# Rotary rotation of query and key tiles in halves of 512 tokens, with three half-size partner buffers

## What is computed

```python
def _layer(x, cond, pl, lambda_init, rope=None, ctx_kv=None):
    ada = (jax.nn.silu(cond) @ pl['w_ada'] + pl['b_ada']).astype(x.dtype)
    sh1, sc1, g1, sh2, sc2, g2 = jnp.split(ada[:, None, :], 6, axis=-1)
    h = x * (1 + sc1) + sh1
    y, k, v = _token_mixers(h, pl, lambda_init, rope, ctx_kv)
...
    z = h @ pl['w_in']
...
def _rot_half(x, cos, sin):
    x1, x2 = jnp.split(x, 2, axis=-1)
    return jnp.concatenate([x1 * cos - x2 * sin, x2 * cos + x1 * sin], -1)
...
        q = _apply_axial_rope(q, rope)
        k = _apply_axial_rope(k, rope)
```

## Time and profile before

| what | value |
|---|---|
| median of 3 runs | 4157.65 us (4147.48 to 4159.18) |
| the profiled execution | 4153.43 us, span 4151.6 us |
| TensorE matmul busy | 3590.7 us (86% of the span) |
| TensorE weight load busy | 2981.8 us (72%) |
| VectorE busy | 2400.7 us (58%) |
| ScalarE busy | 1084.8 us (26%) |
| GpSimd busy | 1542.0 us (37%) |
| mean granted TensorE clock | 0.930 |

### The profile page before, as it was taken

How to read it: one execution, slowest core, us unless ns; L and a number is a source line. 1 busy time by engine, 2 the same in 40 slices (tenths; PEclk the granted TensorE clock), 3 DMA queues, 4 the chain that set the end, 5 groups by cost and what they waited for, 6 DMA issues and landing times. The chain is left out here.

```text
span 4151.6 us, 49240 instructions
## 1 busy us (share of the span) xinstructions
PE 3590.7 (86%) x18590; PEld 2981.8 (72%) x18590; DVE 2400.7 (58%) x2950; ACT 1084.8 (26%) x2000; POOL 1542.0 (37%) x759
## 2 busy tenths in 40 slices
PE   6899897887679999999849997788686999999992
PEld 3577675776568888888737776677565888888882
DVE  3245546775755555555653654677566555555557
ACT  2212112673241111111241111267414111111115
POOL 1526566202423233323344656720133333233234
PEclk7799998998889999999969998999897999999996
DMA  5677544433011111111037654453300111111101
GB/s 201 213 248 214 178 115 158 101 100 107 21 31 36 36 41 41 36 36 41 7 108 229 196 168 138 147 140 99 101 26 21 41 37 35 41 41 32 40 11 51
DMA packets 286902, 380.69 MB, mean 92 GB/s; under 512 B 17743, under 2 KB 203069, under 8 KB 285406
## 3 DMA queue, kind: packets, MB, share of 16 engines
q1 hardware_dynamic: 212370, 219.71, 18.4%
q10 hardware_dynamic: 74316, 157.86, 11.2%
HBM read 286.28 MB, written 82.84 MB: 89 GB/s over the span
## 5 line engine op out<-in xcount | busy, mean ns | idle before, releaser
L665 POOL TENSOR_TENSOR RH<-RAW,ONE 128x1024 fp32r<-128x1024 f32 x256 | 502.2, 1962 | 1805.7 <-PE PS L774 830.2
L774 PE MATMUL PS<-HH,RH 128*128 128x512 f32 (+1 forms) x2784 | 626.1, 369 | 200.6 <-DVE HL L1805 73.7
L774 PEld LDWEIGHTS PS<-HH,RH 128*128 128x128 f32 x2784 | 479.5, 195 | 320.3 <-issue 110.7
L667 POOL TENSOR_TENSOR RL<-RAW,RH 128x1024 fp32r<-128x1024 f32 x256 | 641.2, 2505 | 20.0
L774 PE MATMUL PS<-HL,RH 128*128 128x512 f32 (+1 forms) x2784 | 596.6, 357 | 0.0
L774 PE MATMUL PS<-HH,RL 128*128 128x512 f32 (+1 forms) x2784 | 590.2, 354 | 0.0
L2045 DVE TENSOR_TENSOR SB<-RB 128x512 f32<-128x512 f32 (+1 forms) x192 | 204.2, 1064 | 639.9 <-ACT RB L1688 639.9
L2061 DVE SCALAR_TENSOR_TENSOR XT<-PS,ADA,XT 128x512 f32<-128x512 f32 (+1 forms) x768 | 474.5, 655 | 140.1 <-PE PS L1183 134.7
L774 PEld LDWEIGHTS PS<-HL,RH 128*128 128x128 f32 x2784 | 475.7, 192 | 76.4
L774 PEld LDWEIGHTS PS<-HH,RL 128*128 128x128 f32 x2784 | 469.6, 190 | 72.6
L1688 ACT ACTIVATE RB<-PS 128x512 f32<-128x512 f32 (+1 forms) x192 | 101.2, 527 | 1480.9 <-PE PS L774 1479.7
(11 more groups left out here) (234 smaller groups left out, 5011.1 us busy)
## 6 DMA issues: line engine op xcount, KB each, us to landing
RAW<-in_w_mlp_dram SPq DMA_DIRECT2D x128, 512.0 KB, 3.9
ADW<-in_w_ada_dram ACTq DMA_DIRECT2D x80, 512.0 KB, 5.5
RAW<-const_dram SPq DMA_DIRECT2D x68, 512.0 KB, 3.9
RAW<-in_w_in_dram SPq DMA_DIRECT2D x44, 512.0 KB, 5.1
x_scratch<-XT SPq DMA_DIRECT2D x4, 2560.0 KB, 12.3
z_scratch<-ZST ACTq DMA_DIRECT2D x40, 256.0 KB, 3.2
QH<-q_hi SPq DMA_DIRECT2D x32, 320.0 KB, 9.4
QL<-q_lo SPq DMA_DIRECT2D x32, 320.0 KB, 10.5
```

The lines of the kernel that those rows point to most:

```text
L665: nc.gpsimd.tensor_tensor(RH[:, s, :], RAW[:, p, :], ONE[:].broadcast_to([128, 1024]), ALU.mult).then_inc(hi_split.sem, 1)
L667: nc.gpsimd.tensor_tensor(RL[:, s, :], RAW[:, p, :], RH[:, s, :].bitcast(F32), ALU.subtract)\
L774: mm = pe.matmul(out, w[:, s, k * 128:(k + 1) * 128], m(k), start=(n == 0 and k == 0), stop=(n == 2 and k == KT - 1))
```

## The change

ZSW was one buffer of 1024 tokens; it becomes three of 512. Of every query or key tile the partner features are now moved in two halves, each by eight DMAs of 16 partitions by 512 tokens: the first half after the evacuation of strip q = 0 or 1, in the second strip (that is, right after the second evacuation), the second half after the third strip's. Each group of eight stands ahead of modulation in its strip. GpSimd rotates each half by three operations over 512 tokens. The waits for rotations count halves. Two semaphores are saved elsewhere: the two new_v_stored become one, and a wait on lam_known becomes a link of a chain.

```diff
--- before.py
+++ after.py
@@ -272,7 +272,7 @@
 
     st = Stack(XT_O, WS)
     ZRAW = st.take("ZRAW", [128, 3, T])
-    ZSW = st.take("ZSW", [128, LS])
+    ZSW = st.take("ZSW", [128, 3, 512])
     ZHI = st.take("ZHI", [128, 2, T], F32R)
     ROPE = st.take("ROPE", [128, 2, LS])
     st = Stack(XT_O, WS)
@@ -380,10 +380,9 @@
         c_hi = signal("c_hi", 1)
         c_lo = signal("c_lo", 1)
         c_stored = signal("c_stored", 2 * 16)
-        qk_partner = signal("qk_partner", 8 * 8 * 16)
-        rope_sin = signal("rope_sin", 8)
-        rope_cos = signal("rope_cos", 8)
-        rope_done = signal("rope_done", 8)
+        qk_partner = [signal(f"qk_partner{p}", len(range(p, 16, 3)) * 8 * 16) for p in range(3)]
+        rope_parts = signal("rope_parts", 2 * 16)
+        rope_done = signal("rope_done", 16)
         qk_hi = signal("qk_hi", 8)
         qk_lo = signal("qk_lo", 8)
         zhi_stored = [signal(f"zhi_stored{p}", 4 * 16) for p in range(2)]
@@ -392,7 +391,7 @@
         k_copied = signal("k_copied", 4)
         new_k_stored = [signal(f"new_k_stored{p}", 2 * 16) for p in range(2)]
         v_stored = [signal(f"v_stored{p}", len(range(p, TT, 4)) * 16) for p in range(4)]
-        new_v_stored = [signal(f"new_v_stored{p}", 16) for p in range(2)]
+        new_v_stored = signal("new_v_stored", 2 * 16)
         conv_in = signal("conv_in", 6 * 48 + 2 * 64)
         conv_done = signal("conv_done", 8, 1)
         conv_stored = signal("conv_stored", 8 * 32, 16)
@@ -424,7 +423,6 @@
         hy_stored = signal("hy_stored", 4 * 16, 16)
 
         lam_ready = signal("lam_ready", 1)
-        lam_known = signal("lam_known", 1)
         qk_in = [signal(f"qk_in{s}", 2 * 12 * 16) for s in range(2)]
         v_in = [signal(f"v_in{s}", 2 * 2 * 16) for s in range(2)]
         s_psum = signal("s_psum", 2 * G)
@@ -681,13 +679,16 @@
                 x, z = n % 3, n + 1
                 if n == 0:
                     pool.wait_ge(rope_in.sem, rope_in.at(l, 16))
-                pool.wait_ge(qk_partner.sem, qk_partner.at(l, z * 8 * 16))
-                nc.gpsimd.tensor_tensor(ZSW[:], ZSW[:], ROPE[:, 1, :], ALU.mult).then_inc(rope_sin.sem, 1)
-                nc.gpsimd.tensor_tensor(ZRAW[:, x, 0:LS], ZRAW[:, x, 0:LS], ROPE[:, 0, :], ALU.mult)\
-                  .then_inc(rope_cos.sem, 1)
-                pool.wait_ge(rope_sin.sem, rope_sin.at(l, z))
-                pool.wait_ge(rope_cos.sem, rope_cos.at(l, z))
-                nc.gpsimd.tensor_tensor(ZRAW[:, x, 0:LS], ZRAW[:, x, 0:LS], ZSW[:], ALU.add).then_inc(rope_done.sem, 1)
+                for half in range(2):
+                    u, cols = 2 * n + half, slice(512 * half, 512 * half + 512)
+                    pool.wait_ge(qk_partner[u % 3].sem, qk_partner[u % 3].at(l, (u // 3 + 1) * 8 * 16))
+                    nc.gpsimd.tensor_tensor(ZSW[:, u % 3, :], ZSW[:, u % 3, :], ROPE[:, 1, cols], ALU.mult)\
+                      .then_inc(rope_parts.sem, 1)
+                    nc.gpsimd.tensor_tensor(ZRAW[:, x, cols], ZRAW[:, x, cols], ROPE[:, 0, cols], ALU.mult)\
+                      .then_inc(rope_parts.sem, 1)
+                    pool.wait_ge(rope_parts.sem, rope_parts.at(l, 2 * u + 2))
+                    nc.gpsimd.tensor_tensor(ZRAW[:, x, cols], ZRAW[:, x, cols], ZSW[:, u % 3, :], ALU.add)\
+                      .then_inc(rope_done.sem, 1)
 
             def split_rotated(l, n):
                 x, z = n % 3, n + 1
@@ -1395,17 +1396,19 @@
                             S.activation(to.rearrange("p t v -> p (t v)"), PS[:, 7, 0:8], ACT.Copy)\
                              .then_inc(ada_placed.sem, 1)
 
-                def partners(i):
-
-                    act.wait_ge(z_evac.sem, z_evac.at(l, 3 * (Z_Q + i) + 3))
-                    act.wait_ge(rope_done.sem, rope_done.at(l, i))
+                def partners(i, half):
+
+                    u, cols = 2 * i + half, slice(512 * half, 512 * half + 512)
+                    act.wait_ge(z_evac.sem, z_evac.at(l, 3 * (Z_Q + i) + half + 1))
+                    act.wait_ge(rope_done.sem, rope_done.at(l, max(u - 2, 0)))
                     for p in range(0, 128, 16):
                         o = p + 16 if p % 32 == 0 else p - 16
-                        act.dma_start(ZSW[p:p + 16, :], ZRAW[o:o + 16, i % 3, 0:LS]).then_inc(qk_partner.sem, 16)
+                        act.dma_start(ZSW[p:p + 16, u % 3, :], ZRAW[o:o + 16, i % 3, cols])\
+                           .then_inc(qk_partner[u % 3].sem, 16)
 
                 def high_parts(i):
 
-                    act.wait_ge(rope_done.sem, rope_done.at(l, i + 1))
+                    act.wait_ge(rope_done.sem, rope_done.at(l, 2 * i + 2))
                     act.wait_ge(zhi_stored[i % 2].sem, zhi_stored[i % 2].at(l, 16 * (i // 2)))
                     S.activation(ZHI[:, i % 2, :], ZRAW[:, i % 3, :], ACT.Copy).then_inc(qk_hi.sem, 1)
 
@@ -1467,6 +1470,8 @@
                                 act.wait_ge(zlo_stored[i % 3].sem, zlo_stored[i % 3].at(l, 16 * (i // 3)))
                             S.activation(ZRAW[:, i % 3, t0:t0 + tn], z, ACT.Copy, scale=SCALE if i < HEADS else 1.0)\
                              .then_inc(z_evac.sem, 1)
+                        if i >= 0 and q:
+                            partners(i, q - 1)
                         modulation(u)
                         if q == 0 and i > 1:
                             store_low(i - 2)
@@ -1484,8 +1489,6 @@
                                 prompt_keys(i - HEADS - 1)
                             if i > 0:
                                 high_parts(i - 1)
-                    if i >= 0:
-                        partners(i)
                     if i > 0:
                         store_high(i - 1)
                     if n in UNIT_AT:
@@ -1506,7 +1509,7 @@
                     act.dma_start(v_d[t], VRAW[:, t % 4, :]).then_inc(v_stored[t % 4].sem, 16)
                     if t >= ST:
                         act.dma_start(new_v[0, l, (t - ST) * 128:(t - ST + 1) * 128].rearrange("p m d -> p (m d)"),
-                                      VRAW[:, t % 4, :]).then_inc(new_v_stored[t % 2].sem, 16)
+                                      VRAW[:, t % 4, :]).then_inc(new_v_stored.sem, 16)
 
                 for t in range(TT):
                     keep_value(t)
@@ -1536,7 +1539,7 @@
                     act.wait_ge(u_psum.sem, u_psum.at(l, t + 1))
                     S.activation(MH[:, t, 256:512], PS[:, 4 + t % 2, 0:256], ACT.Copy).then_inc(u_hi.sem, 1)
 
-                for stored in (*v_stored, *new_v_stored):
+                for stored in (*v_stored, new_v_stored):
                     act.wait_ge(stored.sem, stored.at(l, stored.per_layer))
                 for j in range(TT):
                     b0 = 2 * (j % 2)
@@ -1721,7 +1724,7 @@
                 act.wait_ge(y_stored[p].sem, 16 * TT // 2)
             for p in range(2):
                 act.wait_ge(new_k_stored[p].sem, new_k_stored[p].at(DEPTH - 1, 2 * 16))
-                act.wait_ge(new_v_stored[p].sem, new_v_stored[p].at(DEPTH - 1, 16))
+            act.wait_ge(new_v_stored.sem, new_v_stored.at(DEPTH - 1, 2 * 16))
 
 
         @block.vector
@@ -1943,8 +1946,7 @@
 
                 dve.wait_ge(lam_exp.sem, lam_exp.at(l, 1))
                 C.link(V.tensor_tensor(LAMS[:, 0:1], LAMS[:, 3:4], LAMS[:, 2:3], ALU.subtract))
-                V.tensor_tensor(LAMC[:, 2:3], LAMS[:, 0:1], LAMC[:, 0:1], ALU.subtract).then_inc(lam_known.sem, 1)
-                dve.wait_ge(lam_known.sem, lam_known.at(l, 1))
+                C.link(V.tensor_tensor(LAMC[:, 2:3], LAMS[:, 0:1], LAMC[:, 0:1], ALU.subtract))
 
                 def maxima(g, m):
                     h, t, k0, kn = item(g)
```

## The result

| | before | after the change |
|---|---|---|
| median of 9 runs each | 4156.82 us (4147.48 to 4159.37) | 4164.44 us (4159.38 to 4170.47) |
| the profiled execution | 4153.43 us, span 4151.6 | 4159.38 us, span 4157.6 |
| mean granted TensorE clock | 0.930 | 0.930 |
| query and key tiles, layer 0 | 143.0 us | 160.6 us |
| query and key tiles, layer 1 | 135.6 us | 131.9 us |

The ratio to the kernel before is 1.0024, with a 95% interval of 1.0013 to 1.0034: slower by 7.6 us between the medians, a third of the 23 us that were forecast, and inside the 0.3% that I had called no change. Small as it is, the interval leaves out 1, so the loss is real. The last two rows are the stage of the change, from the first matmul of tile 10 to the first of the values (before: 303.6 to 446.6 us and 2302.0 to 2437.6 us). It lost 17.6 us in layer 0 and gained 3.7 us in layer 1.

The account below looks back on a forecast made before the run. TensorE was taken to bound the kernel, its waits coming from ScalarE. Layer 0 +25 us (+19.8 idle, +5 clock) and layer 1 -1 gave +24: 4177 from the profiled execution, 4181.7 from the median, so 4180, range 4150 to 4204.

Parts of the forecast that it names:

- The loop and its end: Query/key tiles: rotation, ZHI, evacuation, issue and landing loop in 16.9 us a tile; the change ends ZHI's 4.5 us wait.
- The issue at 5.0 us a group: ScalarE's issue of eight half-length partner DMAs costs 5.0 us, as at double length, with bounds of 2.8 and 6.3 us.
- Both rivals with a cheaper issue: ScalarE's partner issue: near 0.45 us each, 4158 us, chance 0.2; or 0.35 us each, 4146 us, chance 0.12.
- the estimate of 0.43 us: ScalarE's DMA issue by the skill's 512 cycles at 1.2 GHz: 3.4 us a group, sum near 0.
- The queue did not fill up: Rival on ScalarE's partner groups: 6.3 us each, about +36 us in layer 0, +12 in layer 1, 4204; chance 0.13.
- The places in layer 0: TensorE's idle places at strips 33 to 50: sum 27.0 us plus 2.4 of hand-over, against 9.6 before, +19.8.
- the two of 0.7 us: Layer 0, weights for strip 37 and again after the turn at 46: TensorE waits another 0.7 us each.
- Hand-overs of 2.4 us: Layer 0: about 0.3 us of hand-over added at each of eight places where TensorE waits.
- 0.6 + 5.0: ScalarE in layer 0: an evacuation of 0.6 us, then a group's issue of 5.0, before its other duties.
- 0.6 + 5.0 + 1.2 + 0.4 + 5.0: ScalarE's longer sums: evacuation 0.6, group 5.0, ZHI 1.2, evacuation 0.4, second group 5.0 us, before what TensorE awaits.
- The clock: TensorE in layer 0: 2.5 us lost per idle time of 2.9 us or more, four against two, +5 us.
- within 0.3%: Whole kernel: a difference under 12.5 us can't be told from none; chance 0.20.

Follow-up runs that it names:

- modulation first: The changed kernel with modulation(u) ahead of the group of eight partner DMAs in each strip: 4142.97 us, 0.9967 of the kernel before.
- the same halves without ScalarE's burden: The changed kernel with both partner groups of a tile issued by SyncE, high_parts waiting for the third evacuation: 4128.26 us, 0.9938 of the kernel before.
- groups wait for their own strip: The changed kernel with each group waiting for the evacuation of the strip it stands behind (half + 2 for half + 1): 4184.23 us, 1.0068 of the kernel before.
- the kernel with 16 DMAs a tile: The kernel before with each partner DMA cut in two over its tokens, all sixteen after the third strip: 4203.83 us, 1.0113 of the kernel before.

## Why the prediction was wrong

Wrong in size, right in sign and in cause: the groups' place ahead of the adaLN copies costs time in layer 0, as the run with modulation first shows. Point by point:

- **The loop and its end**: right. ZHI's waits for GpSimd fell from 77.8 to 6.5 us, and the same halves without ScalarE's burden are 28.4 us faster than before.
- **The issue at 5.0 us a group**: right, 611 ns each. Both rivals with a cheaper issue are out, and with them the estimate of 0.43 us from the Trainium skill's "DMA: Bandwidth & Descriptors" and "Advanced Engine Details and Errata": the runs give 611 ns on ScalarE for 16 partitions at 2 KB and at 4 KB a row, and 612 ns for 32 at 2 KB. The queue did not fill up either: the groups of layer 0 took 5.0 to 5.8 us.
- **The places in layer 0**: the eight waits stand where they were forecast; of the ten places priced, the two of 0.7 us had none, six were too large and two too small. Hand-overs of 2.4 us in all had been added.

| place | forecast | the change | groups wait for their own strip |
|---|---|---|---|
| weights, strip 33 | 5.0 | 2.7 | 6.3 |
| placing, strip 35 | 2.0 | 1.6 | 2.2 |
| weights, strip 37 | 0.7 | none | 1.5 |
| turn, strip 38 | 3.1 | 2.9 | 1.9 |
| turn, strip 42 | 4.3 | 3.4 | 5.2 |
| weights, strip 45 | 2.2 | 1.5 | 2.9 |
| turn, strip 46 | 4.7 | 2.8 | 1.8 |
| placing, strip 47 | 2.0 | 2.3 | 5.0 |
| weights, strip 49 | 0.7 | none | none |
| turn, strip 50 | 2.3 | 2.5 | 2.9 |
| hand-overs, transposes | 2.4 | | 0.6 |
| sum | 29.4 | 19.7 | 30.3 |

**The step that failed** is the first number of those sums: "0.6 + 5.0", and in the longer ones "0.6 + 5.0 + 1.2 + 0.4 + 5.0". They count the activations in front of a group as time before it. The group waits only for the strip before, so that its issue runs while the activation still executes: about 0.55 us less at a place with one group, and up to 0.6 + 1.2 + 0.4 = 2.2 us less at those with two. At the turn at 42 it was only 0.8 us less (the row copy ended 12.9 us after strip 40's evacuation began, in place of 13.7), as the first group took 5.8 us there; at strip 33, behind the sigmoid, the group started 1.8 us earlier than in the sum, and the wait was 2.7 in place of 5.0. I had read the wait's number off as that of the group's own strip, as it was in the kernel before. The waits of layer 0 came to 19.7 us in place of 29.4. The last column tests it: with that one number changed they come to 30.3, and the time to 4184 us against 4180 forecast. It bears out the sum more than each place: strip 46 has 1.8 where I had 4.7, strip 47 has 5.0 where I had 2.0. And that 4184 lies so near to 4180 is in part luck: stage 0 of that kernel is 33.2 us longer than before, where I had 25, since beyond work and waits 19.1 us are left in it, 11.6 more than before, where I had 5.

- **The clock**: about right. The work of stage 0 is 127.4 us by the prediction's prices (eight tiles of 13.85, ten rounds, six turns, three transposes). Before, 143.0 less that and 8.1 of idle time leaves 7.5 us; after, 160.6 less that and 19.7 leaves 13.5. The difference is 6.0, where I had 5. The mean granted clock of the stage fell from 0.95 to 0.93.
- **Layer 1**: -1 forecast; the stage lost 3.7 us and the wait of 1.3 before the last transposes went too. The same step failed: the wait before tile 16's transposes is 6.5 us, not 9.7; with the groups waiting for their own strip it is 8.7.
- **What is left**: stages and the two last transposes give 17.6 - 3.7 - 1.5 - 1.3 = +11.1 us between the two profiled executions, whose spans differ by 6.0. The remaining 5 us lie outside, in work the change doesn't touch. Two executions of the kernel before differ by 3 to 4 us at single places as well, so these 5 us may be no effect of the change; that is not shown, and their cause stays open. Of the 18 us by which the profiled execution missed the forecast of +24, some 9 are thus layer 0, 4 layer 1, and 5 are these; the medians are 7.6 us apart.
- **The range** of 4150 to 4204 held the median; the chances did not put enough on "within 0.3%", since the one error of reading ran through every place.

## What to carry to other kernels

Price a group of small DMAs by the engine whose program issues it: here 0.61 us each at 2 KB and at 4 KB a row, and what stands behind them in that program pays. Before you sum an engine's program line by line, read the number in each wait: here an issue that waited for an older result ran under the activation in front of it. And split a transfer only if the first part really leaves earlier, and give the issue to a queue on which nobody waits; here that turned a loss of 7.6 us into a gain of 28.4.

## What the runs showed of the hardware

The issue took 611 ns at 4 KB and 2 KB a row with 16 partitions, and 612 ns with 32 at 2 KB; from SyncE it took 589 at 2 KB. The median landing was 2.8 us at 4 KB; at 2 KB it was 2.4 with the change, 2.0 in the kernel with 16 DMAs a tile and 3.2 from SyncE, so the length isn't all that sets it. I had not expected DMA issues to start 0.06 us after the start of an activation that stands ahead of them in the same program, nor one to start before ZHI, which precedes it in the program (360.76 and 361.06): by these times ScalarE's program had gone on while activations ahead of the issue had yet to end or start. With a wait for the activation just ahead, the issue started 0.62 us after that activation's start in place of 0.06.
